# Beginning of a fused transformer kernel in another order, and one modulation chunk summed over the steps of a loop

## The chip, the cores and the metric

The kernel runs on one core of one Trainium2 chip, in one launch. The metric is the device time of one execution in microseconds; lower is better. Engines are named as in the profile: PE (TensorE, matmuls), DVE (VectorE), ACT (ScalarE), POOL (GpSimd) and SP (SyncE, which here only issues DMAs).

## The reference, cut to what matters

Two transformer blocks run one after the other on 256 tokens of width 1024, all in fp32. The change lies in the beginning of the first block: the modulation, the first norm and the first feed-forward layer.

```python
c_act = jax.nn.silu(c)
for i in range(DEPTH):                                   # 2 layers
    mod = (c_act @ mod_w[i] + mod_b[i])[:, None, :]      # 1024 x 9216
    sh0, sc0, g0, sh1, sc1, g1, sh2, sc2, g2 = jnp.split(mod, N_MOD, axis=-1)
    h = modulate(rms_norm(x, norm_g[i, 0]), sh0, sc0)    # h * (1 + scale) + shift
    x = x + 0.5 * g0 * swiglu(h, ffn_w_gu[i, 0], ffn_w_down[i, 0])
    ...                                                  # mixer, second feed-forward
def swiglu(h, w_gu, w_down):                             # 1024 -> 2 x 2816 -> 1024
    g, u = jnp.split(h @ w_gu, 2, axis=-1)
    return (jax.nn.silu(g) * u) @ w_down
```

## The kernel before

**Products.** Each fp32 matrix is split into a high and a low part. A product is three matmuls: high weights by high activations (line 517), low weights by high activations (518), high weights by low activations (519). ACT makes the high part of a weight piece (`split`, line 1292), DVE the low one (line 1893). A weight piece is 128 x 2048 elements, loaded by two DMAs of 512 KB on SP's queue into one of 3 raw buffers; 6 pairs of split pieces can stand ready. A step of the feed-forward layer is a pass over 256 columns of the gate and 256 of the up projection (`columns`), the gate's silu on ACT (line 1326), the product with the up half on DVE (`product` and `inner`, line 1965), the turn of the result (`turn_one`, `turn_inner`), its high and low part (`hidden_hi`, lines 1485 and 1335; `hidden_lo`, lines 2033 and 1978) and the products with the down projection (`down_block`). The first step (`first_head`) is written out by hand on every engine, a second (`step(0)`) follows, then a loop of 3 turns of two steps, then the last steps.

**Modulation.** The 9216 modulation columns of a layer are worked off in 18 chunks of 512 columns, each (layer, number). A chunk's weights are 2 MB, two DMAs on POOL's queue, each 4 k-tiles (rows of 128). DVE sums a chunk over its 8 k-tiles, one instruction each (`add_chunk`, line 1931 for the first, 1934 for the others); PE turns the sum into a column (`turn_chunk`, line 626, into bank M); DVE reduces it and adds the bias (`keep_turned`, lines 1948 and 1950), which frees the bank. The loop's chunks are worked off so, one for each step, between the halves of `columns`. The first four chunks hold shift and scale of the first norm, so the first product waits for them. Chunks 0 and 1 PE sums itself (`own_chunk`, line 635), and the row goes over ACT (`keep_row`) and `turn_row` (line 644); chunks 2 and 3 DVE sums and `sum_chunk` (line 617) turns them. POOL loads them in the order 2, 0 for the first halves, then the second halves; then 1 and 3.

**The rest of the beginning.** `turn_join` (line 674) turns the normed tokens, half of the width at a time; `scaled_tiles` applies scale and shift (DVE, line 2026, for the first 128 tokens; ACT for the others); `half_hi` (ACT, line 1480) and `x_lo` (DVE, line 2217) split them. `keep_awake` issues transposes whose result nobody reads.

**What sets the order.** Each engine's program is written in its own function, in the order in which it runs; engines wait for each other by counting semaphores. `filled` and `drained` count fills and drains of PSUM banks 4 to 7, named A, B, T and M; `w_hi`, `w_lo` and `w_used` count weight pieces. Where one engine's instruction waits, everything behind it on that engine waits too. In the kernel before, PE's beginning is:

```python
own_chunk(0, 1)
...
turn_row(gate[0:1, :])
turn_join((0,))
sum_chunk()
turn_join((1,))
keep_awake(T, 20)
ffn(0, mod_cols(0, 2))
```

## Time and profile before

| | |
|---|---|
| median of three runs | 1370.38 us (1368.65 to 1371.72) |
| profiled execution | 1369.79 us, span of its profile 1368.1 us |
| PE busy | 1326.5 us, 97% of the span |
| DVE, ACT, POOL busy | 947.8 (69%), 644.0 (47%), 151.6 us (11%) |
| granted clock of PE, mean | 0.996 |
| moved by DMA | 304.82 MB, 223 GB/s in the mean |

The span is shorter than the execution by 1.7 us, which lie around it. "PEclk" is the granted clock of PE as a share of 2.4 GHz: 1.00, or 0.50 where it is at 1.2 GHz. Durations of matmuls overlap, since the next begins before the last has drained. In a timeline, the bracket gives the idle time of the engine before an instruction and what released it.

### The profile page before, as it was taken

To read this page: it belongs to the slowest core of one execution; us is meant where nothing else is said; L and a number is where in the kernel's file an instruction comes from. 1 tells how busy PE (TensorE), PEld (TensorE's weight loads), DVE (VectorE), ACT (ScalarE), POOL (GpSimd) and SP (SyncE) were. 2 spreads that over 40 slices of the span, in tenths; PEclk is the share of its full clock that TensorE was granted. 3 is DMA by queue.
4 is the path that set the end of the run, shared out by engine and by line. 5 is a ranking of instruction groups with operands and counts; after the bars stand their busy time and mean duration, and the time that the engine had idled before them with its cause. 6 is when DMAs were issued, how large, how long until landed. Compare 5 with 4: busy or idle time off the path is not lost.

```text
span 1368.1 us, 17819 instructions
## 1 busy us (share of the span) xinstructions
PE 1326.5 (97%) x6271; PEld 1079.2 (79%) x6271; DVE 947.8 (69%) x1125; ACT 644.0 (47%) x847; POOL 151.6 (11%) x227
## 2 busy tenths in 40 slices
PE   5999999999999999999999899999999999999997
PEld 3678887888888888888778788888887778888885
DVE  3788888779887788887677575465786556554452
ACT  3344334553333643335566643334665664643341
POOL 3110001200010100000231100010126000000000
PEclk9999999999999999999999999999999999999999
DMA  9999887499886698875543395555445444465540
GB/s 334 319 351 345 304 306 259 141 344 309 302 308 230 222 305 314 305 245 177 184 151 127 102 328 167 195 191 177 138 162 201 156 153 132 143 228 190 193 145 31
DMA packets 186070, 304.82 MB, mean 223 GB/s; under 512 B 8524, under 2 KB 134884, under 8 KB 185752
## 3 DMA queue, kind: packets, MB, share of 16 engines
q1 hardware_dynamic: 165432, 224.63, 48.8%
q0 software_dynamic: 20576, 79.37, 16.5%
q8 instruction: 39, 0.64, 0.2%
q14 instruction: 23, 0.19, 0.0%
HBM read 302.91 MB, written 1.05 MB: 222 GB/s over the span
## 4 chain that ended last, share of the span: by engine, by line
PE 83%; DVE 7%; ACT 4%; DMA 3%; issue 2%; POOL 1%; SPq 0%; POOLq 0%; DVEq 0%; ACTq 0%
PE ps L517 25%; PE ps L519 25%; PE ps L518 25%; DVE wlo L1893 2%; ACT whi L1292 2%; DVE arena L1934 2%; DMA raw<-in_ffn_w_gu 1%; DMA arena<-in_mod_w 1%; PE ps L599 1%; PE ps L635 1%; PE ps L626 1%; PE ps L948 1%; PE ps L672 1%; PE ps L970 1%; DMA raw<-in_ffn_w_down 1%
## 5 line engine op out<-in xcount | busy, mean ns | idle before, releaser
L1893 DVE TENSOR_TENSOR wlo<-raw,whi 128x2048 fp32r<-128x2048 f32 x212 | 482.6, 2299 | 97.0 <-ACT whi L1292 94.4
L517 PE MATMUL ps<-whi,nthi 128*128 128x512 f32 (+1 forms) x1264 | 505.8, 400 | 4.8 <-DVE ntlo L2217 2.8
L519 PE MATMUL ps<-whi,ntlo 128*128 128x512 f32 (+1 forms) x1264 | 493.1, 390 | 0.0
L518 PE MATMUL ps<-wlo,nthi 128*128 128x512 f32 (+1 forms) x1264 | 491.9, 389 | 0.0
L1292 ACT ACTIVATE whi<-raw 128x2048 fp32r<-128x2048 f32 x212 | 397.5, 1909 | 81.4 <-DMA raw<-in_ffn_w_gu 27.7
L517 PEld LDWEIGHTS ps<-whi,nthi 128*128 128x128 f32 x1264 | 238.2, 188 | 54.2 <-issue 5.9
L519 PEld LDWEIGHTS ps<-whi,ntlo 128*128 128x128 f32 x1264 | 238.0, 188 | 51.2
L518 PEld LDWEIGHTS ps<-wlo,nthi 128*128 128x128 f32 x1264 | 238.7, 189 | 45.2
L1934 DVE SCALAR_TENSOR_TENSOR arena<-arena,cact 128x512 f32<-128x512 f32 x238 | 178.7, 751 | 10.6 <-DMA arena<-in_mod_w 3.1
L517 PE MATMUL ps<-whi,hthi 128*128 128x512 f32 x440 | 172.7, 393 | 1.5 <-DVE htlo L1984 1.0
L519 PE MATMUL ps<-whi,htlo 128*128 128x512 f32 x440 | 171.6, 390 | 0.0
L518 PE MATMUL ps<-wlo,hthi 128*128 128x512 f32 x440 | 171.3, 389 | 0.0
L1326 ACT ACTIVATE arena<-ps 128x256 f32<-128x256 f32 x110 | 41.8, 382 | 220.7 <-PE ps L519 220.4
L1335 ACT ACTIVATE hthi<-ps 128x512 fp32r<-128x512 f32 x40 | 24.0, 599 | 194.9 <-PE ps L599 194.9
L517 PEld LDWEIGHTS ps<-whi,hthi 128*128 128x128 f32 x440 | 82.6, 188 | 19.0 <-issue 1.6
L519 PEld LDWEIGHTS ps<-whi,htlo 128*128 128x128 f32 x440 | 82.6, 188 | 17.3
L518 PEld LDWEIGHTS ps<-wlo,hthi 128*128 128x128 f32 x440 | 82.6, 188 | 16.7
L2754 POOL DMA_DIRECT2D arena<-in_mod_w x64 | 48.3, 755 | 415.2 <-DVE arena L1934 363.7
L1978 DVE TENSOR_TENSOR htlo<-ps,hthi 128x512 fp32r<-128x512 f32 x40 | 27.6, 690 | 94.5 <-ACT hthi L1335 94.5
L1965 DVE TENSOR_TENSOR arena<-arena,ps 128x256 f32<-128x256 f32 x110 | 43.6, 416 | 56.8 <-ACT arena L1326 56.2
L2790 POOL TENSOR_SCALAR ss<-ss 128x1 f32<-128x1 f32 x18 | 11.2, 625 | 509.2 <-ACT ps L1365 509.2
L1365 ACT ACTIVATE ps<-xres 128x1024 f32<-128x1024 f32 x18 | 18.5, 1027 | 57.6 <-DVE xres L2181 36.7
(276 smaller groups left out, 871.9 us busy)
## 6 DMA issues: line engine op xcount, KB each, us to landing
raw<-in_ffn_w_gu SPq DMA_DIRECT2D x176, 512.0 KB, 5.2
arena<-in_mod_w POOLq DMA_DIRECT2D x72, 1024.0 KB, 6.8
raw<-in_ffn_w_down SPq DMA_DIRECT2D x88, 512.0 KB, 5.5
raw<-in_w_in SPq DMA_DIRECT2D x44, 512.0 KB, 4.6
raw<-in_w_gate_up SPq DMA_DIRECT2D x44, 512.0 KB, 4.8
raw<-in_diff_w_qkv SPq DMA_DIRECT2D x24, 512.0 KB, 4.6
raw<-in_w_down SPq DMA_DIRECT2D x22, 512.0 KB, 5.8
raw<-in_diff_w_o SPq DMA_DIRECT2D x8, 512.0 KB, 4.1
```

The source lines that it names most:

```text
L517: pe.matmul(o, hi, wh, start=start, stop=False)
L518: pe.matmul(o, hi, wl, start=False, stop=False)
L519: return pe.matmul(o, lo, wh, start=False, stop=stop)
L1292: nc.scalar.activation(whi[:, s * PIECE:(s + 1) * PIECE], raw[:, r * PIECE:(r + 1) * PIECE], ACT.Copy).then_inc(w_hi, 1)
L1326: nc.scalar.activation(sil[:, j, :], o[:, 0:FFW], ACT.Silu).then_inc(silu_done, 1)
L1335: nc.scalar.activation(hthi[:, par * BLK:(par + 1) * BLK], o, ACT.Copy).then_inc(ht_hi, 1)
L1365: nc.scalar.activation(junk, x[:, t, :], ACT.Square, accum_out=ss[:, t:t + 1]).then_inc(sq_done, 1)
L1893: v.tensor_tensor(wlo[:, s * PIECE:(s + 1) * PIECE], raw[:, r * PIECE:(r + 1) * PIECE], hi, ALU.subtract).then_inc(w_lo, 1)
L1934: e = v.scalar_tensor_tensor(acc, src[k // 4][:, k % 4, :], cact[:, k:k + 1], acc, ALU.mult, ALU.add)
L1965: v.tensor_tensor(sil[:, j, :], sil[:, j, :], ps[:, b, FFW:2 * FFW], ALU.mult).then_inc(drained[b], 1)
L1978: v.tensor_tensor(htlo[:, at], ps[:, T, :], hthi[:, at].bitcast(F32), ALU.subtract)\
L2754: pool.dma_start(mbuf[mod_place(c.first)][h], src[:, 4 * h:4 * h + 4, bass.ds(chunk * MCH, MCH)])\
```

## The change

The first four chunks are loaded in quarters of 512 KB, two k-tiles each, with a semaphore for each, and chunk 0 now stands ahead of chunk 2 on POOL's queue. SP's first weight piece waits for the last quarter of chunk 0 (before: the last half of chunk 2). PE works through chunk 0 in two halves, with the join's turns between and behind them; `keep_awake` is gone there. The first products run in another order (`both_tokens`: the high weights by the high activations of both token blocks come first), and the order of the first step's banks is T, A, M, B where it was T, M, A, B.

Chunk (0, 5) was summed by `add_chunk` in the first steps. Now it is loaded into the idle buffer `xn`, a megabyte at a time, and DVE adds one k-tile in each step (`slow_add`): one in each of the loop's six, two behind it. For this the loop is unrolled on DVE. PE turns its sum behind the loop's last chunk (`last_chunks`), both in bank M. Chunk (0, 6) takes its place in the first step, and chunk (0, 4) is turned between the halves of that step's columns.

```diff
-        MOD_STEP = [((0, 5), (0, 6)), ((0, 17),), ((1, 7),), ((1, 16),), ()]
+        MOD_SLOW = (0, 5)
+        MOD_STEP = [((0, 6),), ((0, 17),), ((1, 7),), ((1, 16),), ()]
...
-                    load_gu(gu, 0, 0, [(first_landed[2][1], 16)])
+                    load_gu(gu, 0, 0, [(first_landed[0][3], 16)])
                     load_gu(gu, 1, 0)
-                    load_gu(gu, 0, 4, [(first_landed[3][0], 16)])
+                    load_gu(gu, 0, 4, [(first_landed[3][1], 16)])
                     load_gu(gu, 1, 4)
...
-
+            def turn_slow():
+
+                pe.wait_ge(slow_step, KT)
                 o = bank(M)
-                for k in range(KT):
-                    if k % 4 == 0:
-                        pe.wait_ge(first_landed[i][k // 4], 16 * lap)
+                    mm = pe.transpose(o[:, q * P:(q + 1) * P], slow_acc[:, q * P:(q + 1) * P], ident[:, :])
+                mm.then_inc(filled[M], 1)
+
+            def last_chunks():
+                turn_chunk()
+                turn_slow()
+
+            def own_half(i, o, h):
+
+                for k in range(4 * h, 4 * h + 4):
+                    if k % 2 == 0:
+                        pe.wait_ge(first_landed[i][k // 2], 16)
-                    if k == 3:
-                        mm.then_inc(first_used, 1)
-                mm.then_inc(filled[M], 1)
+                mm.then_inc(filled[M] if h else first_used, 1)
...
+                def both_tokens(h, o0, o1):
+                    p = n.next("piece").first
+                    wh, wl = (w[:, p * PIECE:(p + 1) * PIECE].rearrange("p (k n) -> p k n", k=4) for w in (whi, wlo))
+                    pe.wait_ge(w_hi, p + 2)
+                    pe.wait_ge(nt_hi, 2 * h + 1)
+                    one(o0, h, nth, 0, wh, opens=(h == 0))
+                    pe.wait_ge(nt_lo, 2 * h + 1)
+                    one(o0, h, ntl, 0, wh)
+                    pe.wait_ge(nt_hi, 2 * h + 2)
+                    one(o1, h, nth, 1, wh, opens=(h == 0))
+                    pe.wait_ge(w_lo, p + 2)
+                    mm = one(o0, h, nth, 0, wl, closes=(h == 1))
+                    if h:
+                        mm.then_inc(filled[T], 1)
+                    pe.wait_ge(nt_lo, 2 * h + 2)
+                    one(o1, h, ntl, 1, wh)
+                    one(o1, h, nth, 1, wl, closes=(h == 1)).then_inc(w_used, 1)
...
+                t0, a = bank(T), bank(A)
+                both_tokens(0, t0, a)
+                o = bank(M)
+                own_half(1, o, 0)
+                own_half(1, o, 1)
                 w1 = views()
                 b = bank(B)
-                half(b, 1, 0, w1)
+                half(b, 1, 0, w1, (0, 1))
                 turn_row(gate[0:1, :])
+                half(b, 1, 0, w1, (2, 3))
                 sum_chunk()
                 m = bank(M)
                 half(m, 0, 0, w1).then_inc(w_used, 1)
-                w0 = views()
-                pe.wait_ge(nt_lo, 3)
-                half(t0, 0, 1, w0).then_inc(filled[T], 1)
+                both_tokens(1, t0, a)
                 w1 = views()
                 half(m, 0, 1, w1).then_inc(filled[M], 1)
                 turn_one(0, T, T)
-                pe.wait_ge(nt_lo, 4)
-                half(a, 1, 1, w0).then_inc(w_used, 1)
-                turn_one(1, M, M)
+                turn_one(1, A, A)
                 half(b, 1, 1, w1).then_inc(w_used, 1)
-                turn_one(0, A, A)
...
-                step(0, middle=turn_chunk if len(MOD_STEP[f]) == 2 else None,
+                step(0, turn_chunk if f == 0 else None, middle=turn_chunk if len(MOD_STEP[f]) == 2 else None,
...
-                    turn_chunk()
                 else:
                     ffn_head(f)
                 ffn_steps(f)
-                columns(turn_chunk if MOD_LOOP[f] else None)
+                columns(last_chunks if f == 0 else turn_chunk if MOD_LOOP[f] else None)
                 d8 = down_piece()
...
-            own_chunk(0, 1)
+            own = bank(M)
+            own_half(0, own, 0)
             pe.wait_ge(prm_landed, 16 * 9)
             pe.wait_ge(ident_landed, 16)
             o = bank(A)
             pe.transpose(o[:, 0:NROWS], prow[0:NROWS, :], ident[0:NROWS, 0:NROWS])
             pe.transpose(o[:, 128:200], brow[0][:, :], ident[0:72, 0:72])
             pe.transpose(o[:, 256:328], brow[1][:, :], ident[0:72, 0:72]).then_inc(filled[A], 1)
+            turn_first(0, 0)
+            turn_first(0, 1)
+            own_half(0, own, 1)
+            turn_first(1, 0)
             pe.wait_ge(consts_set, 3)
             turn_row(gate[0:1, :])
-            turn_join((0,))
             sum_chunk()
-            turn_join((1,))
-            keep_awake(T, 20)
+            turn_first(1, 1)
...
                 product(0, T)
+                n.next(A)
+                product(1, A)
+                hidden_lo(0, 0, T)
+                split(1)
+                pass_by(M)
+                product(0, M)
+                hidden_lo(0, 1, A)
+                split(1)
                 c = add_chunk(halves=(0,))
-                pass_by(M)
-                product(1, M)
-                hidden_lo(0, 0, T)
-                split(1)
-                n.next(A)
-                product(0, A)
-                hidden_lo(1, 0, M)
-                add_chunk(halves=(1,), of=c)
                 n.next(B)
                 product(1, B)
-                hidden_lo(0, 1, A)
+                hidden_lo(1, 0, M)
                 split(1)
                 hidden_lo(1, 1, T)
-                split(1)
+                add_chunk(halves=(1,), of=c)
+                split(2)
                 keep_turned(chunk_at(*MOD_HEAD[0]))
-                c = add_chunk(halves=(0,))
-                split(1)
-                add_chunk(halves=(1,), of=c)
...
+            def slow_add(k):
+                if k % 4 == 0:
+                    dve.wait_ge(slow_landed[k // 4], 16)
+                if k == 0:
+                    e = v.tensor_scalar(slow_acc, slow_half[:, 0, :], cact[:, 0:1], None, ALU.mult)
+                else:
+                    dve.wait_ge(slow_step, k)
+                    e = v.scalar_tensor_tensor(slow_acc, slow_half[:, k % 4, :], cact[:, k:k + 1], slow_acc, ALU.mult, ALU.add)
+                e.then_inc(slow_step, 1)
             def ffn_steps(f):
...
+                if f == 0:
+
+                    for k in range(2 * TURNS):
+                        step(1 - k % 2, chunk_at(*MOD_LOOP[0]) + 4 * (k - 1))
+                        slow_add(k)
+                    slow_add(2 * TURNS)
+                    slow_add(2 * TURNS + 1)
+                    return
...
                     keep_turned(chunk_at(*MOD_LOOP[f]) + 4 * (2 * TURNS - 1))
+                if f == 0:
+                    keep_turned(chunk_at(*MOD_SLOW))
...
             def load_own_chunk(layer, chunk, i, behind=(), halves=(0, 1)):
                 src = d["mod_w"][layer].rearrange("(k p) n -> p k n", p=P)
                 for h in halves:
                     if behind:
                         pool.wait_ge(*behind[h])
-                    pool.dma_start(mfirst[i][h], src[:, 4 * h:4 * h + 4, chunk * MCH:(chunk + 1) * MCH])\
-                        .then_inc(first_landed[i][h], 16)
+                    for q in (2 * h, 2 * h + 1):
+                        k = 2 * (q % 2)
+                        pool.dma_start(mfirst[i][h][:, k:k + 2, :], src[:, 2 * q:2 * q + 2, chunk * MCH:(chunk + 1) * MCH])\
+                            .then_inc(first_landed[i][q], 16)
...
             for h in range(2):
-                for j in (2, 0):
+                for j in (0, 2):
...
-            load_chunk(*MOD_STEP[0][1])
+            pool.wait_ge(nt_lo, 4)
+            load_slow(0)
             load_loop(0)
+            pool.wait_ge(slow_step, 4)
+            load_slow(1)
             load_chunk(*MOD_NINTH[0])
-            pool.wait_ge(acc_step, 11 * KT)
+            pool.wait_ge(acc_step, 10 * KT)
```

Three places, as the engines now run them against before. In the rows, a line number is that of the kernel in question, and the names in brackets are the semaphores waited for; 4 to 7 behind `filled` and `drained` are the banks A, B, T, M.

The first place is PE, from the first turned row to the first weight product. Before:

```order
L644 MATMUL ps<-ones,gate 128x1 [waits drained7,consts_set]
L644 MATMUL ps<-ones,gate 128x1 x3
L674 MATMUL ps<-rdiag,xres 128x128 [waits rdiag_ready]
L674 MATMUL ps<-rdiag,xres 128x128 x7
L617 MATMUL ps<-ones,arena 128x1 [waits drained7,acc_step]
L617 MATMUL ps<-ones,arena 128x1 x3
L674 MATMUL ps<-rdiag,xres 128x128 [waits rdiag_ready]
L674 MATMUL ps<-rdiag,xres 128x128 x7
L681 MATMUL ps<-ident 128x128 [waits drained6]
L681 MATMUL ps<-ident 128x128 x19
L517 MATMUL ps<-whi,nthi 128x512 [waits nt_lo,w_lo]
```

The changed kernel, from the second half of chunk 0 on:

```order
L650 MATMUL ps<-arena,cact 1x512 [waits first_landed02]
L650 MATMUL ps<-arena,cact 1x512
L650 MATMUL ps<-arena,cact 1x512 [waits first_landed03]
L650 MATMUL ps<-arena,cact 1x512
L689 MATMUL ps<-rdiag,xres 128x128 [waits rdiag_ready]
L689 MATMUL ps<-rdiag,xres 128x128 x3
L657 MATMUL ps<-ones,gate 128x1 [waits drained7,consts_set]
L657 MATMUL ps<-ones,gate 128x1 x3
L621 MATMUL ps<-ones,arena 128x1 [waits drained7,acc_step]
L621 MATMUL ps<-ones,arena 128x1 x3
L689 MATMUL ps<-rdiag,xres 128x128 x4
L755 MATMUL ps<-whi,nthi 128x512 [waits nt_hi,w_hi,drained4]
```

The join's turns (674, now 689) moved ahead of and in between chunk 0's matmuls (650); the 20 transposes are gone; the first product no longer waits for low weights and low activations.

The second place is DVE at the last gated product of the head, for bank B. Before it is the third of the rows at 1965; behind it stands the hidden low part of another bank:

```order
L1965 TENSOR_TENSOR arena<-arena,ps 128x256 [waits silu_done]
L2033 TENSOR_TENSOR htlo<-ps,hthi 128x2x128 [waits ht_hi]
L1893 TENSOR_TENSOR wlo<-raw,whi 128x2048 [waits w_hi]
L1965 TENSOR_TENSOR arena<-arena,ps 128x256 [waits silu_done]
L2033 TENSOR_TENSOR htlo<-ps,hthi 128x2x128 [waits ht_hi]
L1934 SCALAR_TENSOR_TENSOR arena<-arena,cact 128x512 [waits acc_step,mod_landed11]
L1934 SCALAR_TENSOR_TENSOR arena<-arena,cact 128x512 [waits acc_step] x3
L1965 TENSOR_TENSOR arena<-arena,ps 128x256 [waits silu_done]
L2033 TENSOR_TENSOR htlo<-ps,hthi 128x2x128 [waits ht_hi]
L1893 TENSOR_TENSOR wlo<-raw,whi 128x2048 [waits w_hi]
```

Now it is the second of the rows at 2005:

```order
L2073 TENSOR_TENSOR htlo<-ps,hthi 128x2x128 [waits ht_hi]
L1933 TENSOR_TENSOR wlo<-raw,whi 128x2048 [waits w_hi]
L2005 TENSOR_TENSOR arena<-arena,ps 128x256 [waits silu_done]
L2073 TENSOR_TENSOR htlo<-ps,hthi 128x2x128 [waits ht_hi]
L1933 TENSOR_TENSOR wlo<-raw,whi 128x2048 [waits w_hi]
L1971 TENSOR_SCALAR arena<-arena,cact 128x512 [waits mod_landed00]
L1974 SCALAR_TENSOR_TENSOR arena<-arena,cact 128x512 [waits acc_step] x3
L2005 TENSOR_TENSOR arena<-arena,ps 128x256 [waits silu_done]
L2073 TENSOR_TENSOR htlo<-ps,hthi 128x2x128 [waits ht_hi]
L1933 TENSOR_TENSOR wlo<-raw,whi 128x2048 [waits w_hi]
```

A low weight part (1933) and the first half of chunk (0, 4) stand between the products of M and B, where the second half of that chunk stood. The high part that the weight piece needs comes from ACT, at the same place. Before:

```order
L1326 ACTIVATE arena<-ps 128x256 [waits filled7]
L1485 ACTIVATE hthi<-ps 128x2x128 [waits filled6]
L1326 ACTIVATE arena<-ps 128x256 [waits w_used]
L1485 ACTIVATE hthi<-ps 128x2x128 [waits filled7]
L1326 ACTIVATE arena<-ps 128x256 [waits w_used]
L1485 ACTIVATE hthi<-ps 128x2x128 [waits filled4]
L1292 ACTIVATE whi<-raw 128x2048 [waits w_used,raw_landed0]
L1485 ACTIVATE hthi<-ps 128x2x128 [waits filled6]
```

Now the high part (1329 is the split, 1363 the gate's silu, 1522 the hidden high part) stands behind B's gate, and the gates of A and M have changed places:

```order
L1363 ACTIVATE arena<-ps 128x256 [waits w_used]
L1522 ACTIVATE hthi<-ps 128x2x128 [waits filled6]
L1363 ACTIVATE arena<-ps 128x256 [waits filled7]
L1522 ACTIVATE hthi<-ps 128x2x128 [waits filled4]
L1363 ACTIVATE arena<-ps 128x256 [waits w_used]
L1329 ACTIVATE whi<-raw 128x2048 [waits raw_landed2]
L1522 ACTIVATE hthi<-ps 128x2x128 [waits filled7]
L1329 ACTIVATE whi<-raw 128x2048 [waits w_used,raw_landed0]
L1522 ACTIVATE hthi<-ps 128x2x128 [waits filled6]
```

The third place is the columns behind the loop, on PE. Before:

```order
L519 MATMUL ps<-whi,ntlo 128x512
L626 MATMUL ps<-ident,arena 128x128 [waits drained7,acc_step]
L626 MATMUL ps<-ident,arena 128x128 x3
L517 MATMUL ps<-whi,nthi 128x512 [waits w_lo]
L518 MATMUL ps<-wlo,nthi 128x512
```

Now with a second turn, for the slow chunk, which waits for bank M and for the slow sums:

```order
L523 MATMUL ps<-whi,ntlo 128x512
L630 MATMUL ps<-ident,arena 128x128 [waits drained7,acc_step]
L630 MATMUL ps<-ident,arena 128x128 x3
L638 MATMUL ps<-ident,gate 128x128 [waits drained7,slow_step]
L638 MATMUL ps<-ident,gate 128x128 x3
L521 MATMUL ps<-whi,nthi 128x512 [waits w_lo]
L522 MATMUL ps<-wlo,nthi 128x512
```

On DVE it was there:

```order
L1978 TENSOR_TENSOR htlo<-ps,hthi 128x512 [waits ht_hi]
L2112 REGISTER_ALU
L2112 COMPARE_AND_BRANCH
L2201 SCALAR_TENSOR_TENSOR scol<-modc,cols 128x8 [waits drained7]
L2142 ISA [waits dve_chain]
L1893 TENSOR_TENSOR wlo<-raw,whi 128x2048 [waits w_hi] x2
L1948 TENSOR_REDUCE small<-ps 128x4 [waits filled7]
L1950 TENSOR_TENSOR modc<-small,modb 128x4 [waits csum_done]
L1893 TENSOR_TENSOR wlo<-raw,whi 128x2048 [waits w_hi]
```

and is now, with three slow k-tiles ahead and a second pair of rows at 1988 and 1990:

```order
L2018 TENSOR_TENSOR htlo<-ps,hthi 128x512 [waits ht_hi]
L2122 SCALAR_TENSOR_TENSOR gate<-xn,cact,gate 128x512 [waits slow_step] x3
L2258 SCALAR_TENSOR_TENSOR scol<-modc,cols 128x8 [waits drained7]
L2197 ISA [waits dve_chain]
L1933 TENSOR_TENSOR wlo<-raw,whi 128x2048 [waits w_hi] x2
L1988 TENSOR_REDUCE small<-ps 128x4 [waits filled7]
L1990 TENSOR_TENSOR modc<-small,modb 128x4 [waits csum_done]
L1988 TENSOR_REDUCE small<-ps 128x4 [waits filled7]
L1990 TENSOR_TENSOR modc<-small,modb 128x4 [waits csum_done]
L1933 TENSOR_TENSOR wlo<-raw,whi 128x2048 [waits w_hi]
```

The drain of bank M for which the second turn waits is the first row at 1990, behind both weight pieces.

## Rows read from the trace of the kernel before

**Rows 1.** The page, part 1: busy us, share of the span and instructions of each engine.

```profile
PE 1326.5 (97%) x6271; PEld 1079.2 (79%) x6271; DVE 947.8 (69%) x1125; ACT 644.0 (47%) x847; POOL 151.6 (11%) x227
```

**Rows 2.** PE's waits: line waited for, us in total, times, longest us.

```profile
PE ps L635 <- DMA arena<-in_mod_w: 13.1, 1, 13.1
PE ps L626 <- DVE arena L1934: 2.6, 1, 2.6
```

**Rows 3.** PE's timeline, 12 to 45 us: start, us, line, operation, tiles, idle before.

```profile
13.08 9.58 PE L635 MATMUL ps<-arena,cact 128*1 128x512 f32 x16 [13.08 <-DMA arena<-in_mod_w]
...
23.43 1.02 PE L644 MATMUL ps<-ones,gate 1*128 1x1 f32 x8 [0.39 <-ACT gate L1545]
24.38 2.05 PE L674 MATMUL ps<-rdiag,xres 128*128 128x128 f32 x16
...
28.95 2.35 PE L681 MATMUL ps<-ident 128*128 128x128 f32 x20
31.97 0.47 PE L517 MATMUL ps<-whi,nthi 128*128 128x512 f32 x1 [0.68 <-DVE ntlo L2217]
...
37.62 7.03 PE L635 MATMUL ps<-arena,cact 128*1 128x512 f32 x16
```

**Rows 4.** DVE's timeline, 10 to 82 us; the columns of rows 3.

```profile
10.20 0.49 DVE L1931 TENSOR_SCALAR arena<-arena,cact 128x512 f32<-128x512 f32 x1 [10.20 <-DMA arena<-in_mod_w]
...
15.70 3.11 DVE L1934 SCALAR_TENSOR_TENSOR arena<-arena,cact 128x512 f32<-128x512 f32 x4 [2.65 <-DMA arena<-in_mod_w]
...
27.66 1.37 DVE L2026 TENSOR_SCALAR xn<-ps,scol,modc 128x128 f32<-128x128 f32 x4
...
80.97 2.29 DVE L1893 TENSOR_TENSOR wlo<-raw,whi 128x2048 fp32r<-128x2048 f32 x1 [2.74 <-ACT whi L1292]
```

**Rows 5.** ACT's timeline, 22 to 80 us; the columns of rows 3.

```profile
22.70 0.59 ACT L1545 ACTIVATE gate<-ps 1x512 f32<-1x512 f32 x1 [11.93 <-PE ps L635]
...
29.64 1.17 ACT L1480 ACTIVATE nthi<-xn 128x512 fp32r<-128x512 f32 x2
...
79.03 1.92 ACT L1292 ACTIVATE whi<-raw 128x2048 fp32r<-128x2048 f32 x1 [6.67 <-DMA raw<-in_ffn_w_gu]
```

**Rows 6.** Stretches: us, busy of PE, PEld, DVE, ACT, POOL; PEclk, DMA share, GB/s.

```profile
13.00:32.00 19.00, 17.86 (x88) 9.55 (x88) 8.44 (x18) 6.13 (x9) 4.16 (x6) 1.00 1.02 361
47.60:50.90 3.30, 2.00 (x16) 1.85 (x16) 2.06 (x4) 0.00 (x0) 0.00 (x0) 1.00 1.03 360
52.40:55.80 3.40, 3.40 (x9) 2.62 (x8) 1.58 (x4) 3.14 (x4) 0.00 (x0) 0.50 1.02 376
55.80:96.00 40.20, 40.20 (x187) 32.84 (x185) 35.35 (x43) 16.88 (x18) 5.22 (x7) 1.00 0.98 334
96.10:98.70 2.60, 0.04 (x2) 0.05 (x1) 2.49 (x5) 1.91 (x1) 0.00 (x0) 1.00 0.98 394
98.70:219.00 120.30, 120.30 (x557) 99.57 (x558) 103.27 (x115) 46.30 (x42) 11.05 (x16) 1.00 0.93 321
```

**Rows 7.** Groups by shape, 13 to 217 us: count, busy, mean ns; idle before, releaser.

```profile
L1893 DVE TENSOR_TENSOR wlo<-raw,whi 128x2048 fp32r<-128x2048 f32 x33 | 74.9, 2289 | 15.0 <-ACT whi L1292 14.9
...
L1934 DVE SCALAR_TENSOR_TENSOR arena<-arena,cact 128x512 f32<-128x512 f32 x82 | 61.6, 751 | 5.2 <-DMA arena<-in_mod_w 2.7
...
L1326 ACT ACTIVATE arena<-ps 128x256 f32<-128x256 f32 x20 | 7.5, 383 | 36.1 <-PE ps L519 36.1
...
L2217 DVE TENSOR_TENSOR ntlo<-xn,nthi 128x512 fp32r<-128x512 f32 x4 | 2.6, 688 | 0.8 <-ACT nthi L1480 0.8
```

**Rows 8.** DVE's timeline, then PE's, at the loop's end; the columns of rows 3.

```profile
197.76 0.69 DVE L1978 TENSOR_TENSOR htlo<-ps,hthi 128x512 fp32r<-128x512 f32 x1 [1.37 <-ACT hthi L1335]
...
199.56 4.49 DVE L1893 TENSOR_TENSOR wlo<-raw,whi 128x2048 fp32r<-128x2048 f32 x2 [1.04 <-ACT whi L1292]
203.97 0.68 DVE L1948 TENSOR_REDUCE small<-ps 128x4 f32<-128x512 f32 x1
...
202.42 0.60 PE L626 MATMUL ps<-ident,arena 128*128 128x128 f32 x4
```

81 lines of the change are left out of this document (44 added, 37 removed).

## The prediction, made before the changed kernel was run

> **What bounds the kernel now.** I read the page first. TensorE (PE) is busy 97% of the span [rows 1], so a change can pay only where PE stands still or runs slowly, and costs wherever it makes PE wait. The list of PE's waits, largest first, then gives the places. Beyond the 13.1 us before the first matmul the longest stop of the whole program is the 2.6 us one, for VectorE's (DVE) modulation sums [rows 2], and it lies in the part that is edited. The timeline of PE from 12 us on shows the beginning [rows 3]: chunk 0's own matmuls run from 13.08 to 22.66, and the first weight matmul stands only at 31.97. Between them lie short jobs and 20 transposes whose result nobody reads: a chain of hand-overs, not work. The table of stretches tells the rest [rows 6]: 1.30 us of idle in 47.6 to 50.9, a stretch of 3.40 us at granted clock 0.50 (1.2 GHz) behind it, the 2.6 us stop, and then 120.30 busy us of 120.30 through the feed-forward loop. The DMA share is 1.02 from 13 to 32 us and 0.98 to 1.03 in the stretches from 47.6 to 98.7, so weights that PE asks for earlier need not be there earlier.
>
> All terms below are PE's time, made against the profiled execution, 1369.79 us, which lies 0.59 below the median of the three runs shown.
>
> **What is taken away.**
>
> 1. The start of the weight matmuls. Chunk 0 was second in each pair on POOL's queue; now it is first, in quarters. The pair's first half lands at 10.20 and the second pair's first at 15.70 (when DVE got chunk 2's) [rows 4]. At the 361 GB/s of that stretch [rows 6] a quarter, 0.52 MB, takes 1.45 us, so chunk 0's first should land near 8.8, and its last at 15.7. PE's sixteen own-chunk matmuls took 9.58 us in the first pass and 7.03 in the second, warm one [rows 3]; I take 9.58. Two of the four join blocks now lie inside (a quarter of the 2.05 + 2.03 us each, so 1.0), and the parameter transposes (0.7 together): the own chunk ends at 8.8 + 9.58 + 1.7 = 20.1, give or take a microsecond. Then ACT's copy of the row 0.59 [rows 5], turning the row 1.02 [rows 3], the column sums about 1.0, DVE's two small additions and the scale about 0.4, the scaled tiles 1.37 [rows 4], and half of ACT's 1.17 for two halves [rows 5]: 0.6. The other two join blocks lie beside ACT's and DVE's part of this. PE starts at about 25.1, where before it was 31.97, since the first product now wants the high part alone, and not the two 2 us pieces of DVE ahead of it. **−6.9.**
> 2. The same reordering at the second half of the tokens (own chunk 1, row, sums): the 1.30 us of idle between 47.6 and 50.9 [rows 6] lies behind products now. **−1.4.**
> 3. The 2.6 us stop at 96 to 98.7 [rows 2, 6]: its chunk, (0,5), is no longer summed before the loop. **−2.6.**
> 4. The stretch at half clock, 52.4 to 55.8: 3.40 us did 1.7 us of full-speed work [rows 6], so it cost 1.7. It comes after a stretch with 2.00 busy us of 3.30, of tiny matmuls. That stretch gets denser, but the beginning becomes as thin: the 20 transposes that kept PE busy for 2.35 us [rows 3] are gone, and 20.1 to 25.1 holds some 3 us of tiny matmuls. **0**, with bounds −1.7 and +1.7.
>
> The Trainium skill, "TensorE: Matmul & The Clock Gate", section "What's actually happening", has a rule against the removal: the throttled state is the default, and only activity releases it. By it the start loses what the later stretch gains, the sum stays as it stands; without it the sum would be 1.7 lower. The row at clock 0.50 agrees [rows 6]; the 96.1 row, 2.6 us idle at 1.00 with no fall behind it, does not by itself.
>
> **What is added.**
>
> 5. Small waits of the new order: PE has twelve products, 2.7 us, ahead of the first that wants the low weights, and DVE needs 0.65 + 2.29 us [rows 7] for them: 0.35. The product of bank M comes about 0.6 late. **+1.0**, bounds 0 and 2.
> 6. The last gated product of the head, product(1, B). On ACT, the high part of piece 5 now stands behind that block's gate; on DVE its low part and half a chunk (four k-tiles) stand ahead of the product. From the end of PE's block b: gate 0.38 [rows 7], ACT's high part 1.92 [rows 5], DVE's low part 2.29, the half chunk 0.48 + 3 x 0.751 = 2.7 [rows 7], the product, a row of the same size as the gate, 0.4: 7.9 us with hand-overs. PE has 2 transposes and 12 products to do meanwhile, 14 x 120.30/557 = 3.0 [rows 6], and about half a microsecond of waiting in it: 3.5. Then turn_one(1, B) stops PE, and behind it on PE's queue stand all products of the first down block's second half and the first step. In the kernel before, the half chunk stood there too, but no weight piece, and PE didn't stop. **+4.4**, bounds 3 and 5.5.
> 7. Clock after that stop. The 2.6 us stop between dense products cost no clock, the 1.30 us among thin ones did [rows 6]; this stop is longer than both. **+1.6** of the 1.7 that such a stretch costs; bounds 0 and 1.7.
> 8. The first step's columns. Terms 1 to 7 bring PE there about 3.9 us sooner. Pieces 8 and 9 land when the queue allows: ACT waited 6.67 us for piece 8 until 79.03, DVE behind it until 80.97 [rows 4, 5]. If they land as before, PE waits all 3.9; if the megabyte taken from this queue helps (2.7 us at 361 GB/s [rows 6]) it waits little. Nothing in the trace shows which; I take **+3**, nearer the row, bounds 0 and 3.9.
> 9. Half clock after that stop: **+0.8**, bounds 0 and 1.7.
> 10. last_chunks. The loop's chunk and the slow one are turned back to back into one bank, M, so PE's second turn waits for DVE to take the first. DVE's last low part of the loop ends at 198.45 [rows 8]. Then come three slow k-tiles (the last step's and two more), 3 x 0.751 + hand-overs = 2.4, the scale 0.15, two low pieces 4.5, the reduction 0.68 with its addition 0.2 [rows 7, 8]: 206.3. PE is there at 202.42 + 0.4 [rows 8], so it waits 3.5, and with it the second half of the columns. The DMAs of the slow chunk (two of 1 MB on POOL's queue, the first now ahead of the loop's loads) have some 17 us until they are read: nothing. **+3.6**, bounds 2.5 and 4.5.
> 11. Half clock after that stop: **+0.8**, bounds 0 and 1.7.
>
> Costed at nothing: the other slow k-tiles, one of 0.75 us a step, each behind the low part of the hidden rows, in which DVE was idle 1 us and more before its next piece [rows 8]; without this cover each is 0.75 on a 17 us step. The moved turn of the HEAD chunk: as many matmuls as before. The unrolled DVE loop: same instructions.
>
> Sum: −6.9 − 1.4 − 2.6 + 0 + 1.0 + 4.4 + 1.6 + 3 + 0.8 + 3.6 + 0.8 = **+4.3**, so 1374.1; with half the distance to the median 1374.3. What is given at the start is eaten at the head's end and at the first step, and the turn after the loop is a loss by itself.
>
> **The rivals.**
>
> A, the other side: a stop of PE costs only its own length, and gives the queue time to catch up. Then 7, 8, 9 and 11 are nothing, the start keeps its clock (term 4 is −1.7), and the sum is −10.9 − 1.7 + 1.0 + 4.4 + 3.6 = −3.6: 1366.2. For it: the 2.6 us stop at full clock. Against: the half-clock row after a shorter idle. It decides once 7, 8, 9 and 11 together come to less than 1.9 of the 6.2 with term 4 at 0.
>
> B: pieces come no earlier, and every stop brings a full slow stretch: 4 at +1.7, 8 at +3.9, 9 and 11 at 1.7 each: +8.7, 1378.5.
>
> C, nothing comes of the start: the beginning is bound by transfers (share 1.02 [rows 6]). The stops at 6 and 8 are then no additions, they are where the gain is given back, and the loop starts earlier only by the missing megabyte, 2.7. With 10 on top: +0.9, 1370.7, the clock left aside.
>
> D: quarters of 512 KB travel slower than 1 MB loads. The rows give 361 GB/s for the stretch of mixed sizes and 334 later [rows 6]; the first four chunks' 8 MB at the lower rate take 25.1 us where they took 23.2: +1.9, 1376.2. The Trainium skill, "DMA: Bandwidth & Descriptors", section "Bandwidth", says to batch DMAs to 1 MiB or more, which speaks against quarters; that no run here shows at this size. In the rows, SP's pieces of 512 KB go in the same stretch as POOL's loads of 1 MB at that rate, so D gets little.
>
> **How the numbers follow.** Forecast 0.48, with an own range of 1372 to 1376.5; A 0.14; B 0.13; C 0.20; D 0.05. A measurement of this kernel tells about 0.2% (2.74 us) from no change: bounds 1367.6 and 1373.1. Slower: the forecast but for its low end (0.42), B and D (0.17): 0.59. Same: C and that low end, 0.27. Faster: A, 0.14. The likeliest is 1374.3. The range takes in C, D and B's bulk and leaves A's far end and B's last bit out: 1367.5 to 1378.5.
>
> **What would show it.** Term 1: the first line-521 or 755 product near 25. Terms 2, 3: no stop of PE over 0.5 us at the sums and none for (0,5). Term 6: a PE wait of about 4 us for the line 2005 product of bank B; if it is under 2, the step is wrong and A gains. Term 8: a second stop ten to twenty microseconds later, for DVE's hidden low part. Terms 4, 7, 9, 11: stretches at 0.50 in the table, which none would refute. Term 10: a wait of about 3.5 us at line 638, for bank M. A loop without stops that begins more than 5 us earlier would make the forecast wrong.

## The result, and the profile after

The changed kernel takes 1381.23 us in the median (1378.86 to 1382.5, four runs) where the kernel before took 1371.05 in the runs beside it: a ratio of 1.0073, 95% interval 1.0057 to 1.0089. It is about 10 us slower, clear of the 0.2% that can be told. The sign was forecast, the size was not: 1374.3 was said, and the range ended at 1378.5. The profiled execution took 1378.86 us, 9.1 over that of the kernel before. It is the fastest of the four: its mean granted clock is 0.990, that of the other three 0.987, and no profile shows where those lost the difference.

The page of the changed kernel, PE's row of part 1 and the clock of part 2:

```profile
PE 1330.4 (97%) x6251; PEld 1082.4 (79%) x6251; DVE 948.0 (69%) x1125; ACT 643.6 (47%) x847; POOL 156.4 (11%) x235
...
PEclk9989999999999999999999999999999999999999
```

PE's share is what it was [rows 1]; the clock shows one 8 among the first slices. PE's waits, those that changed; the columns are those of rows 2:

```profile
PE ps L650 <- DMA arena<-in_mod_w: 8.6, 1, 8.6
PE ps L612 <- DVE arena L2005: 5.5, 3, 4.0
PE ps L603 <- DVE arena L2005: 4.8, 1, 4.8
PE ps L638 <- DVE modc L1990: 3.2, 1, 3.2
...
PE ps L755 <- ACT nthi L1517: 1.6, 1, 1.6
```

The first wait is 4.5 us shorter, as planned, and the 2.6 us stop at line 626 [rows 2] is gone. Four new ones take their place: for the product of bank B (4.0 of the 5.5), for the first step's product (4.8), for bank M behind the loop (3.2), and 1.6 for ACT at the first product. The stretches, columns as in rows 6:

```profile
26.00:31.70 5.70, 5.68 (x13) 4.45 (x14) 5.34 (x4) 3.70 (x6) 2.48 (x4) 0.50 0.99 346
47.00:50.00 3.00, 3.00 (x15) 2.47 (x14) 2.20 (x6) 3.00 (x7) 1.51 (x2) 1.00 0.19 22
69.30:72.70 3.40, 3.40 (x10) 2.62 (x9) 3.36 (x4) 2.03 (x2) 0.44 (x1) 0.50 1.03 381
90.30:95.10 4.80, 0.00 (x0) 0.01 (x1) 4.69 (x8) 1.99 (x3) 0.09 (x1) 0.80 0.97 304
95.10:100.00 4.90, 4.88 (x14) 4.04 (x15) 4.83 (x5) 3.75 (x3) 0.66 (x1) 0.50 1.02 340
100.00:207.60 107.60, 107.60 (x500) 88.85 (x498) 94.43 (x108) 42.86 (x38) 10.09 (x14) 1.00 0.92 320
994.30:1001.10 6.80, 6.80 (x26) 6.03 (x27) 3.62 (x15) 3.00 (x5) 0.00 (x0) 0.50 1.04 386
```

In 26 to 31.7 PE ran at clock 0.50, and again behind each of the first two long stops. From 100 to 207.6 it has no gap, as the loop had none before. In 47 to 50 the transfers all but rest: share 0.19, where the kernel before had 1.04 in the same three microseconds. The last stretch lies far behind the edit; it is spoken of at the end.

Around bank B's product, ACT's rows and then DVE's:

```profile
60.96 0.38 ACT L1363 ACTIVATE arena<-ps 128x256 f32<-128x256 f32 x1 [2.04 <-PE ps L523]
61.24 1.90 ACT L1329 ACTIVATE whi<-raw 128x2048 fp32r<-128x2048 f32 x1
...
63.18 2.29 DVE L1933 TENSOR_TENSOR wlo<-raw,whi 128x2048 fp32r<-128x2048 f32 x1 [1.49 <-ACT whi L1329]
65.39 0.54 DVE L1971 TENSOR_SCALAR arena<-arena,cact 128x512 f32<-128x512 f32 x1
65.96 2.33 DVE L1974 SCALAR_TENSOR_TENSOR arena<-arena,cact 128x512 f32<-128x512 f32 x3
68.20 0.41 DVE L2005 TENSOR_TENSOR arena<-arena,ps 128x256 f32<-128x256 f32 x1
```

The gate is ready at 61.3, the high part of the piece at 63.1, its low part at 65.5, the half chunk at 68.3, and only then comes the product. That is the chain of term 6, step by step. Around the first step's product, again ACT's rows and then DVE's:

```profile
84.00 1.92 ACT L1329 ACTIVATE whi<-raw 128x2048 fp32r<-128x2048 f32 x1 [12.67 <-DMA raw<-in_ffn_w_gu]
87.35 1.92 ACT L1329 ACTIVATE whi<-raw 128x2048 fp32r<-128x2048 f32 x1 [1.43 <-DMA raw<-in_ffn_w_gu]
...
89.30 2.29 DVE L1933 TENSOR_TENSOR wlo<-raw,whi 128x2048 fp32r<-128x2048 f32 x1 [0.26 <-ACT whi L1329]
91.51 0.48 DVE L1971 TENSOR_SCALAR arena<-arena,cact 128x512 f32<-128x512 f32 x1
92.03 2.33 DVE L1974 SCALAR_TENSOR_TENSOR arena<-arena,cact 128x512 f32<-128x512 f32 x3
94.27 0.75 DVE L2005 TENSOR_TENSOR arena<-arena,ps 128x256 f32<-128x256 f32 x2
```

ACT waited 12.67 us for its piece, until 84.00 (before: 79.03, [rows 5]). The next piece's low part ends at 91.5, then the half chunk takes 2.75 us, and the product stands behind it at 94.27. PE's turn of that product, before and after:

```profile
90.01 0.60 PE L599 MATMUL ps<-ident,arena 128*128 128x128 f32 x4
...
95.12 1.09 PE L603 MATMUL ps<-ident,arena 128*128 128x128 f32 x4 [4.82 <-DVE arena L2005]
```

PE came there at 90.30 (95.12 less the 4.82 of the wait), 0.3 us later than before: of the earlier start nothing was left at this place, and the stop is the lateness of the piece and of DVE behind it. Ahead of that piece stand loads of POOL. Their issue, before and after:

```profile
60.78 2.23 POOL L2754 DMA_DIRECT2D arena<-in_mod_w  x3 [13.26 <-ACT whi L1292]
...
63.44 1.49 POOL L2811 DMA_DIRECT2D arena<-in_mod_w  x2 [13.78 <-ACT whi L1329]
64.92 0.75 POOL L2817 DMA_DIRECT2D xn<-in_mod_w  x1
```

Both kernels issue three megabytes there, the changed one 2.7 us later: POOL waits for one of ACT's high parts, which began at 58.57 before and now stands behind bank B's gate, at 61.24. Piece 8 is split 18.3 us behind POOL's first issue before and 20.6 us after. Over the runs with all bytes this distance is 20.1 to 20.9 us in the ten profiles that load the slow chunk without holding its loads back, and 18.3 and 18.0 in the two without it (the kernel before, and the run that moves only a sum in it). So of the 5.0 us, 2.7 go with the later issue and 2.3 with the slow chunk's loads. That is read from rows; no run moved this high part on ACT.

At the loop's end, DVE's rows and then PE's last turn of a chunk in the loop:

```profile
203.04 2.32 DVE L2122 SCALAR_TENSOR_TENSOR gate<-xn,cact,gate 128x512 f32<-128x512 f32 x3
...
205.48 4.49 DVE L1933 TENSOR_TENSOR wlo<-raw,whi 128x2048 fp32r<-128x2048 f32 x2
209.89 0.69 DVE L1988 TENSOR_REDUCE small<-ps 128x4 f32<-128x512 f32 x1
210.61 0.16 DVE L1990 TENSOR_TENSOR modc<-small,modb 128x4 f32<-128x4 f32 x1
...
207.10 0.60 PE L630 MATMUL ps<-ident,arena 128*128 128x128 f32 x4
```

PE turned the loop's chunk at 207.10, 4.7 us later than before (202.42, [rows 8]), and waited for the drain of bank M at 210.6. The bytes that the two kernels had moved by 100 us, before and after:

```profile
DMA packets 17156, 33.48 MB, mean 335 GB/s; under 512 B 973, under 2 KB 11605, under 8 KB 17151
...
DMA packets 16859, 31.84 MB, mean 318 GB/s; under 512 B 1072, under 2 KB 11704, under 8 KB 16855
```

At the 0.34 MB per us of the first of these rows, 1.64 MB are 4.8 us, about as much as the loop's end is late. That the one makes the other, these two rows alone do not show.

### The profile page after: what moved, and what is told of

It reads as the page before. It is cut to its first block, busy times and chain, and to the rows that moved or that the text cites. A ratio compares the mean times of both kernels' runs of the same rounds, so it can differ in the third digit from the quotient of the medians.

```text
span 1377.2 us, 17684 instructions
## 1 busy us (share of the span) xinstructions
PE 1330.4 (97%) x6251; PEld 1082.4 (79%) x6251; DVE 948.0 (69%) x1125; ACT 643.6 (47%) x847; POOL 156.4 (11%) x235
## 4 chain that ended last, share of the span: by engine, by line
PE 86%; DVE 6%; ACT 4%; DMA 2%; issue 1%; POOL 0%; SPq 0%; POOLq 0%; DVEq 0%; ACTq 0%
PE ps L521 26%; PE ps L523 25%; PE ps L522 25%; DVE wlo L1933 2%; ACT whi L1329 2%; PE ps L603 1%; DMA raw<-in_ffn_w_gu 1%; PE ps L755 1%; DVE arena L1974 1%; PE ps L630 1%; PE ps L650 1%; PE ps L982 1%; DMA arena<-in_mod_b 1%; PE ps L680 1%; PE ps L1004 1%
## 5 line engine op out<-in xcount | busy, mean ns | idle before, releaser
L521 PE MATMUL ps<-whi,nthi 128*128 128x512 f32 (+1 forms) x1248 | 499.8, 400 | 4.2 <-DVE ntlo L2274 2.1
L523 PE MATMUL ps<-whi,ntlo 128*128 128x512 f32 (+1 forms) x1248 | 487.1, 390 | 0.0
L522 PE MATMUL ps<-wlo,nthi 128*128 128x512 f32 (+1 forms) x1248 | 486.1, 389 | 0.0
L523 PEld LDWEIGHTS ps<-whi,ntlo 128*128 128x128 f32 x1248 | 235.1, 188 | 50.5
L522 PEld LDWEIGHTS ps<-wlo,nthi 128*128 128x128 f32 x1248 | 235.9, 189 | 44.6
L1974 DVE SCALAR_TENSOR_TENSOR arena<-arena,cact 128x512 f32<-128x512 f32 x231 | 173.6, 751 | 11.6 <-DMA arena<-in_mod_w 3.9
```

Of the source, the lines that this page charges most:

```text
L521: pe.matmul(o, hi, wh, start=start, stop=False)
L522: pe.matmul(o, hi, wl, start=False, stop=False)
L523: return pe.matmul(o, lo, wh, start=False, stop=stop)
L1974: e = v.scalar_tensor_tensor(acc, src[k // 4][:, k % 4, :], cact[:, k:k + 1], acc, ALU.mult, ALU.add)
```

## The experiments

All times are ratios to the kernel before from runs on the same chip. The changed kernel stands at 1.0073, and its interval (1.0057 to 1.0089) must be borne in mind: single repairs of 1 or 2 us are not told apart by time, but by their stops.

**Each new stop undone alone.** The product of bank B ahead of what was put before it:

```diff
+                n.next(B)
+                product(1, B)
                 split(1)
                 c = add_chunk(halves=(0,))
-                n.next(B)
-                product(1, B)
```

> The changed kernel, but on VectorE the product for bank B stands ahead of piece 5's low part and the half chunk. Order theory (each new stop of TensorE comes from what was put ahead on VectorE): the 3.99 us stop at the turn of bank B falls under 0.7 us, the half-clock stretch behind it goes too, the later stop for the first step's product keeps its 4.8, and the time is 4 to 5.7 us below the changed kernel's 1381.2. Transfer theory (the queue runs 1 to 1.5 MB behind, and the pieces for the first step land at 84 to 87 us whatever TensorE does before): the gain comes back as a longer stop for the first step's product, 8 to 9 us instead of 4.8, and the time is within 1.5 us of 1381.2.

Measured 1.0054 (1.0037 to 1.0071). The 4 us stop is gone, and another has grown. PE's largest wait, and ACT's row at the first step's piece:

```profile
PE ps L603 <- DVE arena L2005: 9.0, 1, 9.0
...
83.58 1.92 ACT L1329 ACTIVATE whi<-raw 128x2048 fp32r<-128x2048 f32 x1 [16.25 <-DMA raw<-in_ffn_w_gu]
```

The stop for the first step's product is 9.0 us instead of 4.8: what was gained came back, since the piece lands at 83.6 as it did at 84.0. The order set the stop at bank B; it did not set the end.

The first step's product ahead of its half chunk:

```diff
                     split(1)
-                    c = add_chunk(halves=(0,))
                     inner()
+                    c = add_chunk(halves=(0,))
```

> The changed kernel, but in the first step VectorE takes the gated product ahead of the half chunk, not behind it. Order theory: the half chunk (0.48 + 3 x 0.75 = 2.7 us) leaves the path, the 4.82 us stop falls to about 2.1, and with a shorter half-clock stretch the time is 2.7 to 4.4 us lower than 1381.2. Transfer theory: the same 2.1 us remain, and are the late landing's; if the landing decides alone, the stop stays at 4 or more and the time within 1.5 us of 1381.2.

Measured 1.0061 (1.0044 to 1.0079). The stop there fell to 0.6 us, and the next turn of a chunk, which needs that sum, got one:

```profile
PE ps L630 <- DVE arena L1974: 2.5, 1, 2.5
```

So the half chunk had been on the path, but 2.5 of the 4.3 us won are paid 7 us later.

The slow chunk turned behind the columns, and taken by DVE behind the next product:

```diff
-                columns(last_chunks if f == 0 else ...)
+                columns(turn_chunk if MOD_LOOP[f] else None)
+                if f == 0:
+                    turn_slow()
...
```

> The changed kernel, but the slow chunk is turned behind the columns' second half, and VectorE takes it behind the next gated product. Bank theory (TensorE waits only for the one bank): the 3.2 us stop is gone, at most 1 us of it comes back at the next gated product, and the time is 2.2 to 3.2 us lower than 1381.2. VectorE theory (three slow k-tiles ahead of the weight pieces make VectorE late anyway): the stop moves to the next gated product, 2.5 us or more, and the time is within 1 us of 1381.2.

Measured 1.0024 (1.0006 to 1.0041). The 3.2 us stop is gone, no new one over 0.35 us follows it before 250 us. Of the three new stops this is the one whose repair was not paid back, and the bank theory holds. By the medians the gain is 6.7 us, more than the stop. Of the 4.8 us between the two profiled executions, 3.2 are the stop. Another 1.5 were won before the loop's last turn (205.6 for 207.1), where the edit changes nothing: at the start the clock was at 0.50 for 3.4 us in this run and for 6.8 us in the changed kernel, with the same instructions.

Pieces 2 and 3 split some 5 us sooner on ACT and DVE, so that the raw buffers come free:

```diff
                 keep_own_chunk(chunk_at(*MOD_FIRST[1]))
+                split(1)
                 keep_chunk(chunk_at(*MOD_FIRST[3]))
...
```

> The changed kernel, but ScalarE and VectorE split pieces 2 and 3 some 5 us earlier, so that their raw buffers come free for the next loads near 46.5 us and not at 51.9. Transfer theory: the DMA share in 47 to 50 us rises from 0.19 to over 0.8, piece 8 lands at 79 to 80 and not at 84.0, the stop for the first step's product falls from 4.8 to 2 or less, and the time is 2.5 to 4.5 us lower than 1381.2. Order theory: the pieces land earlier, but the stops at bank B (4.0) and for the slow chunk (3.2) stay, the first step's loses at most 1 us, and the time is 0 to 1.5 us lower.

Measured 1.0058 (1.0041 to 1.0075). The stretch 47 to 50 of this kernel, and its wait:

```profile
47.00:50.00 3.00, 3.00 (x15) 2.48 (x14) 2.20 (x6) 2.48 (x6) 1.51 (x2) 1.00 0.80 212
...
PE ps L603 <- DVE arena L2004: 4.6, 1, 4.6
```

The queue worked where it had rested (0.80 instead of 0.19), piece 8 still came at 84.2, and the stop kept 4.6 us. The early idle time of the queue is not what made piece 8 late: by 51 us this run had moved 15.93 MB against 15.17, by 65 us only 20.12 against 20.01, and POOL's loads were issued at 63.53, as late as in the changed kernel.

**The beginning.** Sixteen transposes put back:

```diff
             turn_row(gate[0:1, :])
+            keep_awake(T, 4)
             sum_chunk()
             turn_first(1, 1)
+            keep_awake(T, 12)
```

> The changed kernel with 16 transposes nobody reads put back into the beginning, 4 ahead of the column sums and 12 ahead of the first weight product. Clock theory (the thin stretch without them is why the granted clock falls to 0.50 at 25 us): no stretch at 0.50 before 50 us, the first 24 products take about 5.5 us and not 8.0, own chunk 1 ends some 2.5 us earlier. Start theory (idle and small matmuls count alike): the stretch at 0.50 stays. In both cases the pieces for the first step land when they did, so the whole gains 0 to 2 us against 1381.2, not more.

Measured 1.0038 (1.0018 to 1.0057). The stretches from 22.6 to 31.7 of this kernel:

```profile
22.60:25.90 3.30, 3.30 (x31) 3.26 (x30) 1.80 (x7) 1.47 (x2) 3.30 (x5) 1.00 0.95 299
26.00:31.70 5.70, 5.39 (x24) 4.08 (x23) 4.95 (x4) 4.18 (x7) 2.08 (x3) 1.00 0.96 321
```

The clock stayed at 1.00, and the first 24 products took the 5.5 us that they should; PE came to bank B 2 us sooner (62.7 instead of 64.7), and to the first step's product as well. Against the expectation piece 8 also came 2.1 us sooner (81.9), with POOL's loads issued at 61.49 and not 63.44, so the stop there kept 4.5 us. The removed transposes were worth their place: in all five runs with them put back the clock was at 1.00 from 20 to 44 us, in all eight with the new beginning and without them it was at 0.50 for 3.4 or 6.8 us near 25 us. The Trainium skill, "TensorE: Matmul & The Clock Gate", section "What's actually happening", says that the throttled state is the default and activity releases it; the two traces agree.

Halves of 1 MB instead of quarters, chunk 0 still first (`first_landed` waited for by halves):

> The changed kernel, but the first four chunks come in halves of 1 MB, still chunk 0 first. Quarter theory (quarters let TensorE begin sooner and cost nothing on the queue): first matmul at 10.2 us and not 8.6, first weight product 0 to 1.5 us later, whole 0 to +1.5 us against 1381.2. Rate theory (quarters travel slower): the chunks' last bytes land 0.5 us or more earlier, the weight pieces too, and the whole is 1 to 2 us faster.

Measured 1.0057 (1.0039 to 1.0075). The first matmul came at 10.0 us and the first weight product at 28.1 instead of 26.0, with 6.30 MB moved by 20 us against 6.24. So quarters are worth 1 to 2 us at the start and cost the queue nothing that these bytes tell, and nothing of it is seen at the end: the interval overlaps the changed kernel's.

**The second part alone.** The slow chunk put into the kernel before, whose beginning stays:

```diff
-        MOD_STEP = [((0, 5), (0, 6)), ...
+        MOD_SLOW = (0, 5)
+        MOD_STEP = [((0, 6),), ...
```

> The kernel before with the second part of the change alone: its beginning is as it was, chunk (0,5) is summed over the loop, and its turn stands behind the loop's last chunk in the same bank. If the loss of the changed kernel lies in its beginning and in the one bank: the 2.56 us stop at 96 us goes, a stop of 3.2 us at the end of the loop comes, and the time is within 1.5 us of before. If the slow k-tiles in the loop or their loads are what costs: stops within the loop, and 3 to 6 us over before.

Measured 1.0032 (1.0022 to 1.0042). PE's waits:

```profile
PE ps L638 <- DVE modc L1968: 3.2, 1, 3.2
...
PE ps L630 <- DVE arena L1952: 2.5, 1, 2.5
```

The stop that term 3 had promised away is still there, with chunk (0, 5) gone. It was not that chunk's. And with the slow chunk's turn apart:

> As the run with the second part alone on the kernel before, but with the slow chunk turned behind the columns and taken behind the next gated product. If only the bank cost: no stop at the end of the loop, the 2.56 us stop at 96 us gone as well, and the time 2 to 3.5 us under before. If the three slow k-tiles make VectorE late there: a stop of 1 to 2.5 us at the next gated product, and the time within 1.5 us of before.

Measured 1.0010 (0.9997 to 1.0022), with no stop behind the loop. Neither branch came true: the gain did not come, and there was no stop at the next product. Spreading the chunk over the loop by itself is worth nothing that can be told, and costs nothing that can be told once its turn is apart.

**Loads held back.** POOL's slow and loop loads wait until piece 7 is split:

```diff
             pool.wait_ge(nt_lo, 4)
+            pool.wait_ge(w_hi, 9)
             load_slow(0)
```

> The changed kernel, but POOL holds the slow chunk's first megabyte, and the loop's first loads behind it, until ScalarE has split piece 7 (71 us), instead of issuing them at 65 to 69 us, just ahead of pieces 8 and 9. Queue theory (those two megabytes are what makes piece 8 land at 84.0): piece 8 lands by 79 us, the 4.82 us stop for the first step's product falls under 2, the 6.8 us at half clock behind it shorten, and the time is 3 to 7 us under 1381.2. Order theory (the half chunk ahead of that product is the cause): piece 8 lands earlier, but the stop keeps 3.5 us or more, since turning the chunk before it sets when VectorE can start, and the time is within 1.5 us of 1381.2.

Measured 1.0025 (1.0008 to 1.0042). PE's wait and ACT's rows at pieces 8 and 9:

```profile
PE ps L603 <- DVE arena L2005: 2.7, 2, 2.1
...
75.95 1.92 ACT L1329 ACTIVATE whi<-raw 128x2048 fp32r<-128x2048 f32 x1 [4.22 <-DMA raw<-in_ffn_w_gu]
84.56 1.92 ACT L1329 ACTIVATE whi<-raw 128x2048 fp32r<-128x2048 f32 x1 [6.69 <-DMA raw<-in_ffn_w_gu]
```

Piece 8 comes at 75.9 instead of 84.0, and the stop is 2.1 us instead of 4.8. Piece 9, which is issued just behind the held loads, lands at 84.6, where it had come at 87.35. So the bytes ahead of a piece decide when it comes. This repair paid as well: its interval lies below the changed kernel's, and PE's last turn of a chunk in the loop came at 204.0 instead of 207.1. The 2.1 us that are left stand behind piece 9.

All five repairs (bank B, first product, turn apart, transposes, hold):

> The changed kernel with five repairs at once: the product for bank B ahead of the low part and the half chunk, the first step's product ahead of its half chunk, the slow chunk turned behind the columns, 16 transposes put back into the beginning, and POOL's loads held back until piece 7 is split. If each stop is its own cause and the queue has room for pieces 8 and 9: no stop over 1.5 us from the beginning to the end of the loop, the loop's end some 10 us sooner than in the kernel before, and the time 5 to 10 us under the kernel before. If the gain is bound by transfers: the stop for the first step's product comes back with 4 to 9 us, and the time is within 3 us of the kernel before.

Measured 1.0016 (1.0003 to 1.0030). No stop at bank B or behind the loop, and 7.7 us for the first step's product, with piece 9 at 85.6. The transfer branch of the expectation holds.

**Two more of term 3 and of bytes.** The five repairs, with pieces 2 and 3 sooner, the hold until piece 8, and the first step's whole chunk behind its product:

> The changed kernel with its repairs, and POOL's slow and loop loads held back until piece 8 is split (some 78 us), pieces 2 and 3 split 5 us sooner, and the first step's whole chunk summed right behind its product. Queue theory: piece 9 lands by 80 us, no stop over 1.5 us from the beginning to the end of the loop, the loop's end 6 to 10 us sooner than in the kernel before, the time 4 to 9 us under it. Order theory (something else than bytes sets when pieces 8 and 9 come): the stop for the first step's product keeps 4 us or more, and the time is within 3 us of the kernel before.

Measured 1.0035 (1.0019 to 1.0052). PE's largest wait:

```profile
PE ps L603 <- DVE arena L2008: 11.1, 1, 11.1
```

Piece 9 now landed at 77 us, and the first step ran without a stop over 1.1 us; a step later one of 11.1 us paid it all back. POOL issued the held loads, three megabytes, from 76.5 to 78.9 us, and that step's pieces were issued from 78.5 on and came at 98.5 and 101.5.

The kernel before with nothing but chunk (0, 6)'s sum moved:

```diff
-                    c = add_chunk(halves=(0,))
+                    add_chunk()
                     split(1)
                     inner_lo(0)
-                    add_chunk(halves=(1,), of=c)
```

> The kernel before with one edit: chunk (0,6)'s second half summed right behind its first half, ahead of the low parts. If VectorE's order caused the 2.56 us stop at 96 us: it falls under 0.7 and the time is 2 to 3.5 us under before. If its second half lands too late (92.7 us in the kernel before): the stop moves onto that landing, at most 1 us is gained, and the low parts behind it come late.

Measured 1.0031 (1.0017 to 1.0046). PE's largest new wait, and ACT's row there:

```profile
PE ps L599 <- DVE arena L1965: 6.0, 1, 6.0
...
105.29 1.92 ACT L1292 ACTIVATE whi<-raw 128x2048 fp32r<-128x2048 f32 x1 [7.23 <-DMA raw<-in_ffn_w_down]
```

The 2.56 us stop is gone, so it was this chunk's sum behind DVE's low parts. But the low part of the next piece ended 2.6 us later, so its raw buffer and the load into it came later, and PE stopped 6.0 us at the next step. The same edit with the slow chunk apart:

> The kernel before with the slow chunk turned apart, and chunk (0,6)'s second half summed ahead of the low parts. If the 2.5 us stop at 96 us came from that order: it is gone, and the time is 2.5 to 4.5 us under the run with the slow chunk apart, so 1 to 3 us under the kernel before. If the chunk's bytes or the bank set it: the stop stays at 2 us or more and the time within 1 us of that run.

Measured 1.0035 (1.0019 to 1.0052): the stop at 96 us went, one of 5.8 us came at 107.6. The first branch had foretold a gain; it came out as a loss both times.

Three repairs that add no bytes, four with the early split, and the hold in the kernel before:

> The changed kernel with three repairs: the slow chunk turned apart (measured alone: its 3.2 us stop goes), transposes back in the beginning (measured alone: no half clock at the start, two us sooner at bank B) and POOL held to piece 7 (measured alone: the 4.8 us stop falls to 2.1). If they add up: loop's end 1 to 2 us later than in the kernel before or equal to it, time within 2 us of the kernel before. If transfers pay the gain back: the stop for the first step's product is 4 us or more again and the time 3 to 5 us over the kernel before.

Measured 1.0014 (1.0003 to 1.0025); the stops at bank B and at the first step's product were 4.6 and 4.5 us, as the transfer branch said, with piece 9 at 86.2, but the time is under that branch's 3 us.

> As the run with three repairs, with pieces 2 and 3 split 5 us sooner, which lets the queue work in 47 to 50 us. If the bytes by 51 us decide: 0.5 MB more by then, 1 to 2 us less than the run with three repairs. If what stands ahead of pieces 8 and 9 decides: within 1 us of that run.

Measured 1.0014 (1.0005 to 1.0024): the second branch, the same time as with three.

> The kernel before with the slow chunk alone, turned apart, and POOL's slow and loop loads held until piece 7 is split. If the loads ahead of pieces 8 and 9 cost there too: 1 to 3 us under the kernel before. If the kernel before has time in hand at that place (no stop at the first step's product): within 1 us of the run with the slow chunk apart without the hold, so 0 to 3 us over the kernel before.

Measured 1.0001 (0.9989 to 1.0013). This is the second branch, at its lower end. No version beat the kernel before; this one equals it.

**The bytes taken away.** In both kernels three quarters of the later modulation bytes are left out, with all instructions kept (the loop over k-tiles reads one tile four times):

```diff
-  pool.dma_start(mbuf[...][h], src[:, 4 * h:4 * h + 4, ...])
+  pool.dma_start(mbuf[...][h][:, 0:1, :], src[:, 4 * h:4 * h + 1, ...])
```

> The changed kernel, but every modulation chunk behind the first four loads one k-tile of each half and not four, and VectorE sums that one four times: as many instructions, a quarter of the bytes, so the modulation it works out is another. Bytes theory: pieces 8 and 9 land by 78 us, the stop for the first step's product falls under 1.5 us; the 4.0 us stop at bank B and the 3.2 us one behind the loop stay, being order. Compared with the kernel before under the same cut: 1 to 5 us slower. Order theory: the 4.8 us stop keeps 3.5 us or more.

Measured 1.0035 (1.0018 to 1.0052). PE's longest waits but the first, ACT's rows at pieces 8 and 9, and PE's last turn in the loop:

```profile
PE ps L612 <- DVE arena L2005: 5.4, 3, 3.9
PE ps L638 <- DVE modc L1990: 3.2, 1, 3.2
...
73.02 1.92 ACT L1329 ACTIVATE whi<-raw 128x2048 fp32r<-128x2048 f32 x1 [1.46 <-DMA raw<-in_ffn_w_gu]
77.69 1.92 ACT L1329 ACTIVATE whi<-raw 128x2048 fp32r<-128x2048 f32 x1 [2.75 <-DMA raw<-in_ffn_w_gu]
...
199.65 0.60 PE L630 MATMUL ps<-ident,arena 128*128 128x128 f32 x4
```

> The kernel before under the same cut of bytes (one k-tile of each half of the later modulation chunks is loaded and summed four times). It is the yardstick for the cut changed kernel. Its 2.56 us stop at 96 us is VectorE's order and stays at 2 us or more; if it was the landing's it falls under 1. Its time is within 6 us of the kernel before: TensorE has no other stop that bytes set up to 250 us.

Measured 0.9999 (0.9986 to 1.0011). PE's rows at the stop of 96 us and at the last turn in the loop:

```profile
97.10 0.65 PE L626 MATMUL ps<-ident,arena 128*128 128x128 f32 x4 [0.96 <-DVE arena L1934]
...
200.88 0.60 PE L626 MATMUL ps<-ident,arena 128*128 128x128 f32 x4
```

With the same instructions and a quarter of those bytes, pieces 8 and 9 come at 73.0 and 77.7, and the 4.8 us stop for the first step's product is gone altogether, half chunk or not. The stops at bank B (3.9) and for bank M (3.2) stay: they are order. With the bytes cut the changed kernel reaches the loop's last turn 1.2 us sooner than the kernel before (199.65 against 200.88), where uncut it is 4.7 us later. So with the bytes out of the way the new beginning is the faster one for PE, by 1.2 us at that turn, and with them, in this order, the slower one. The bytes are not the whole loss: by the ratios the cut gives the changed kernel back some 5 of its 10 us, give or take 3, and leaves it about 4 us behind the kernel before under the same cut (1.0035 against 0.9999). Of these, 3.2 are the stop for bank M, which lies behind that turn. The kernel before wins 1.5 us there by the cut and nothing that its time can tell. Its stop at 96 us fell from 2.56 to 0.96, between the two branches: part order, part bytes.

## Why the prediction was wrong

By the profile of the changed kernel, term by term, in us:

| term | forecast | measured | from |
|---|---|---|---|
| 1 earlier start | −6.9 | −6.0 | first product at 26.02, not 25.1; PE waited 1.6 for ACT's high part |
| 2 sums of the second half | −1.4 | −1.1 | |
| 3 stop at 96 us | −2.6 | −2.6 | gone, but not for the reason given |
| 4 half clock at the start | 0 | +1.2 | 5.7 us at 0.50 cost 2.9; before it cost 1.7 |
| 5 small waits | +1.0 | +0.6 | |
| 6 product of bank B | +4.4 | +4.0 | |
| 7 clock behind it | +1.6 | +1.7 | 3.4 us at 0.50 |
| 8 first step's product | +3 | +4.8 | |
| 9 clock behind it | +0.8 | +2.5 | 4.9 us at 0.50 |
| 10 bank M behind the loop | +3.6 | +3.2 | |
| 11 clock behind it | +0.8 | 0 | in this profile the loop goes on at 1.00 |
| sum | +4.3 | +8.3 | 9.1 between the profiled executions |

From 1374.3 to the measured 1381.23 are 6.9 us: 4.0 from the terms, 0.8 that they leave open, and 2.4 by which the median lies over the profiled execution, less the 0.2 that the forecast had added towards the median of the kernel before.

Right were the terms read from one chain of rows: 1 in its mechanism, 6 and 10 in mechanism and size. The run with the product moved and the one with the turn apart showed each to be order on DVE, and the repair of term 10 was not paid back. In term 1 two errors nearly cancel: the two join blocks inside chunk 0's matmuls took 2.0 us, a quarter of 4.08 each, where the sum had 1.0 for both, and those matmuls took 8.5 and not 9.58. The own chunk so ended at 19.9, as forecast (20.1), and the chain behind it took 6.1 us and not 5.0. Term 11 is 0 by luck of this profile: of the nine profiles with that stop of 3.2 us, five show no fall of the clock behind it, three 3.4 us at 0.50 and one 6.8.

The step that failed first is term 8, in its mechanism and by its bound. It had PE come 3.9 us sooner to pieces that land as before at the worst, and so held the stop at 3.9 at most. PE did not come sooner: the 3.9 counts in term 3's 2.6 us, which lie behind this place (the stop stood at 96 us, this turn at 90.01), and by the measured terms ahead of it nothing was left of the start (90.30 for 90.01). The pieces did not land as before: piece 8 came 5 us later (84.00 for 79.03), behind POOL's loads, which came out later and with the slow chunk's among them, and DVE's half chunk stood ahead of the product as well, which the sum did not count. That its 3 came as near to 4.8 as it did is luck. The run with POOL's loads held (2.1 us), the one with the product ahead of its half chunk (0.6) and the one with the bytes cut (gone) show both parts. Term 9 and its bound went with it: the clock stayed down for 4.9 us of work, where one stretch of 3.4 had been taken for the most. These two make 3.5 of the 4 us missing; term 4, at its upper half, makes another 1.2.

Term 3 was right only in its number. The stop was not chunk (0, 5)'s but chunk (0, 6)'s, whose second half DVE summed behind two low parts. In the changed kernel PE stopped 4.8 us shortly before and found that sum ready. Whether the stop would have stood without that one is not settled: with the product ahead of its half chunk 2.5 us of it came back, with the bytes cut none did.

Of the rivals, B (pieces late, a full slow stretch behind each stop) gave 1378.5 and came nearest, with 0.13. C named a mechanism that the run with bank B's product moved shows, where the start's gain is given back through the transfers; in the changed kernel itself stops and clock ahead of that place had used the gain up. And C put its price at the missing megabyte, where the queue came to 100 us with 1.64 MB less done. D fell: quarters cost nothing that can be told. A fell in the first stretches: the clock went to 0.50 behind both stops.

What stays open: the 0.8 us between the sum and the two executions, in which the clock far behind the edit has 1.7; where the other three executions lost their 2 to 4 us more; and whether some order of loads could keep the gain of the start. Each order tried left or moved the stop (7.7 and 11.1 us in the two runs with all repairs), but none moved the high part on ACT for which POOL's loads wait.

## What to carry to other kernels

Where an engine is at 97% and the DMA share is 1.0 over the same stretch, a stop of that engine may be where the queue catches up: price an earlier start by when each later piece can land, so by the bytes ahead of it and by what their issue waits for, and not only by the stops that it removes. Count at each place only what was won ahead of it. A cheap test is to cut the bytes and keep the instructions: a stop that vanishes needed those bytes, though order may have had its part in it, and one that stays is order. And when two results go through one bank back to back, the second waits for whatever its reader has queued ahead of the first.

## What was not expected of the hardware

A stop of PE cost its clock at some places and not at others: 2.56 us at 96 us in the kernel before left it at 1.00 [rows 6], as did 3.2 us behind the loop in the changed kernel, while behind 4.0 and 4.8 us it was at 0.50 for 3.4 and 4.9 us. In the runs, a stop that costs no clock at one time cost it at another (behind the loop: 6.8 us at 0.50 with the transposes put back, none in the changed kernel; the stop of 2.5 us at chunk (0, 6)'s sum: 3.4 us in the two runs with the slow chunk alone, none in the kernel before).

Far behind the edit the clock falls in some profiled executions and not in others, with the same instructions there: the changed kernel had 6.8 us at 0.50 from 994 us on (the stretch above), the kernel before 3.4 us at 684, and two of the experiments neither. PE's products follow each other by 0.43 us at 0.50 and by 0.23 at 1.00, so about half of such a stretch is lost, and these alone move the time by 1.7 to 5 us from run to run, which is more than most repairs here were worth. It is not the edits: the kernel before alone, in the runs beside the experiments, had a mean granted clock from 0.992 (1373.96 us) to 0.999 (1367.5 us).
